# Queries' square sums as 32-column products, their roots through memory, first decay sums from a built table

## What is computed

```python
def rms_norm(x, g):
    y = xf * lax.rsqrt(jnp.mean(xf * xf, axis=-1, keepdims=True) + EPS)
    return (y * g.astype(jnp.float32)).astype(x.dtype)

# gated_deltanet
    g = -jnp.exp(a_log.astype(f32)) * jax.nn.softplus(a.astype(f32) + dt_bias.astype(f32))
    gcum = jnp.cumsum(gch, axis=-1)
    decay = jnp.exp(jnp.where(incl, gcum[..., :, None] - gcum[..., None, :], -jnp.inf))
...
# dsa_attention
    q = apply_rope(rms_norm(q.reshape(Bsz, T, B_HEADS, B_DH), q_norm), cos_a, sin_a)
    k = apply_rope(rms_norm(k.reshape(Bsz, T, 1, B_DH), k_norm), cos_a, sin_a)[:, :, 0]
```

## Time and profile before

| | us |
|---|---|
| median of 3 runs | 1572.85 |
| the three runs | 1573.34, 1567.5, 1572.85 |
| the profiled execution | 1569.99 |
| its span, first to last instruction | 1568.0 |
| TensorE busy in it | 1555.1 (99%) |
| VectorE busy | 1146.8 (73%) |
| ScalarE busy | 882.9 (56%) |
| mean granted TensorE clock | 0.997 |

### The profile page before, as it was taken

The page is one execution under the profiler, slowest core; times in us unless marked ns, Lnnn a source line. Parts: engine busy times, 40 slices in busy tenths (PEclk is TensorE's granted clock), DMA queues, the critical chain, the costliest instruction groups (busy, mean ns, idle before and its releaser), DMA issues.

```text
span 1568.0 us, 34689 instructions
## 1 busy us (share of the span) xinstructions
PE 1555.1 (99%) x12704; PEld 1522.7 (97%) x12704; DVE 1146.8 (73%) x1901; ACT 882.9 (56%) x1380; POOL 50.4 (3%) x44
## 2 busy tenths in 40 slices
PE   9999999999999999999999999999999999999999
PEld 8999899999999998999999999999999999999999
DVE  7779787766568697786765678888666757678864
ACT  6665656555455756565554565666544456466552
POOL 0100001000000000010000000000010000100000
PEclk9999999999999999999999999999999999999999
DMA  6754154655546541547655545565555545656664
GB/s 217 221 154 122 55 188 150 194 173 173 175 148 181 156 148 63 162 156 223 197 182 191 180 122 186 158 191 187 190 185 184 165 135 162 188 161 189 186 192 131
DMA packets 272878, 263.54 MB, mean 168 GB/s; under 512 B 19440, under 2 KB 271120, under 8 KB 272784
## 3 DMA queue, kind: packets, MB, share of 16 engines
q1 hardware_dynamic: 271552, 258.47, 53.0%
q0 software_dynamic: 944, 3.70, 0.8%
q10 hardware_dynamic: 288, 0.07, 0.0%
HBM read 256.38 MB, written 3.11 MB: 165 GB/s over the span
## 4 chain that ended last, share of the span: by engine, by line
PE 86%; DVE 8%; ACT 3%; issue 1%; DMA 1%; SPq 0%; DVEq 0%; ACTq 0%
PE lin L573 23%; PE lin L576 23%; PE lin L581 23%; PE aux L925 6%; PE lin L925 3%; PE lin L627 3%; DVE wL L560 2%; PE lin L598 1%; PE lin L662 1%; DMA stage<-in_w_in 1%; DVE cT L2100 1%; DVE nT L2545 1%; DVE nL L2550 1%; ACT wH L551 1%; PE aux L576 1%
## 5 line engine op out<-in xcount | busy, mean ns | idle before, releaser
L551 ACT ACTIVATE wH<-stage 128x1024 fp32r<-128x1024 f32 x488 | 493.4, 1049 | 465.6 <-PE lin L576 318.6
L560 DVE TENSOR_TENSOR wL<-stage,wH 128x1024 fp32r<-128x1024 f32 x488 | 575.7, 1223 | 133.5 <-PE lin L581 67.2
L573 PE MATMUL lin<-nH,wH 128*128 128x256 f32 (+2 forms) x2256 | 559.4, 286 | 1.8 <-DVE u L2491 1.5
L576 PE MATMUL lin<-nL,wH 128*128 128x256 f32 (+2 forms) x2256 | 555.1, 285 | 0.0
L573 PEld LDWEIGHTS lin<-nH,wH 128*128 128x128 f32 x2256 | 426.1, 189 | 5.3 <-issue 2.1
L576 PEld LDWEIGHTS lin<-nL,wH 128*128 128x128 f32 x2256 | 427.1, 189 | 0.4 <-issue 0.2
L581 PE MATMUL lin<-nH,wL 128*128 128x256 f32 (+2 forms) x2256 | 295.1, 283 | 0.0
L581 PEld LDWEIGHTS lin<-nH,wL 128*128 128x128 f32 x2256 | 281.4, 188 | 0.3
L573 PE MATMUL lin<-aH,wH 128*128 128x256 f32 (+1 forms) x704 | 172.3, 284 | 0.0
L576 PE MATMUL lin<-aL,wH 128*128 128x256 f32 (+1 forms) x704 | 172.2, 284 | 0.0
L573 PEld LDWEIGHTS lin<-aH,wH 128*128 128x128 f32 x704 | 132.8, 189 | 0.0
(11 more groups left out here) (394 smaller groups left out, 2055.9 us busy)
## 6 DMA issues: line engine op xcount, KB each, us to landing
stage<-in_w_up SPq DMA_DIRECT2D x88, 512.0 KB, 4.5
stage<-in_ffn_w_up SPq DMA_DIRECT2D x88, 512.0 KB, 4.2
stage<-in_w_in SPq DMA_DIRECT2D x52, 512.0 KB, 5.0
stage<-in_w_down SPq DMA_DIRECT2D x40, 512.0 KB, 3.6
stage<-in_ffn_w_down SPq DMA_DIRECT2D x40, 512.0 KB, 4.1
stage<-in_w_gate SPq DMA_DIRECT2D x32, 512.0 KB, 4.7
stage<-in_even_w_in SPq DMA_DIRECT2D x24, 512.0 KB, 4.6
stage<-in_w_out SPq DMA_DIRECT2D x16, 512.0 KB, 4.1
```

What stands on the lines that cost most here:

```text
L551: nc.scalar.activation(wH[:, s, ks, 0:n], stage[:, s, ks, 0:n], ACT.Copy).then_inc(sem["whi"], 1)
L560: nc.vector.tensor_tensor(wL[:, s, ks, 0:n], stage[:, s, ks, 0:n], wH[:, s, ks, 0:n].bitcast(F32), ALU.subtract).then_inc(sem["wlo"], 1)
L573: mm = nc.tensor.matmul(banks[b][0:rows_, 0:width], wH[:, s, k, cols], xh, start=start and n == 0, stop=False)
L576: mm = nc.tensor.matmul(banks[b][0:rows_, 0:width], wH[:, s, k, cols], xl, start=False, stop=False)
```

## The change

In `JOBS` the four names `sbq0` to `sbq3` become one, `sbq`: four products with 32 columns of ones, whose results lie in four groups of 32 partitions of one bank. ScalarE takes one logarithm and one exponential of that bank (into `root_late`), then the key's logarithm, then issues a DMA that stores one row per head into memory (`rows_b`), then the key's exponential. GpSimd waits for that store and issues a DMA that reads the four rows back into all 128 partitions of `rnb[:, 0:4]` (`spread`), ahead of its cosine product of the key. VectorE scales the queries behind `joined(4)`, the split and `masked(5)`, after a wait for that DMA (`roots_b`). For gb0, VectorE builds `gtri0`, the triangle times each head's `gg`, and TensorE runs one product with ones over its 64 columns.

```diff
-    + [f"sbq{h}" for h in range(4)] + ["sbk"] + ["Y_4"] + [x for b in range(3) for x in (f"kt{b}", f"vt{b}")]
+    + ["sbq", "sbk", "Y_4"] + [x for b in range(3) for x in (f"kt{b}", f"vt{b}")]
...
+            def spread(to, rows_, stored, landed):
+
+                pool.wait_ge(*stored)
+                pool.dma_start(to.rearrange("p h t -> p (h t)"), bass.AP(rows_, 0, [[0, P], [1, to.shape[1] * to.shape[2]]])).then_inc(sem[landed], 16)
...
                 for n, (kind, x) in enumerate((("i", rawT[:, 20:24, META:T]), ("i", ikr[:, :].unsqueeze(1)), ("a", bkr[:, :].unsqueeze(1)), ("a", rawT[:, 16:20, :]))):
+                    if n == 2:
+                        spread(rnb[:, 0:4, :], rows_b, (sem["stored_b"], at("stored_b", l, 16)), "roots_b")
...
+                def rows_of_squares(name, x):
+
+                    ps = begin(name, l)
+                    for h in range(4):
+                        t = mm(ps[32 * h:32 * h + 32, 0:T], ones[:, 0:32], x[:, h, :])
+                    t.then_inc(filled(name), 1)
...
+                    if b == 0:
+                        pe.wait_ge(sem["gt"], at("gt", l, 2))
+                        mm(ps[:, 0:4 * n], ones[0:n, :], gtri0.rearrange("p h c -> p (h c)")).then_inc(filled("gb0"), 1)
+                        return
...
-                for h, name in enumerate([f"sbq{h}" for h in range(4)] + ["sbk"]):
-                    mm(begin(name, l)[:, 0:T], ones, sq_att[:, h, :]).then_inc(filled(name), 1)
+                rows_of_squares("sbq", sq_att[:, 0:4])
+                mm(begin("sbk", l)[:, 0:T], ones, sq_att[:, 4, :]).then_inc(filled("sbk"), 1)
...
+                def rows_stored(to, x, n, counter):
+                    act.wait_ge(sem["roots"], at("roots", l, n))
+                    act.dma_start(bass.AP(to, 0, [[T, 4], [1, T]]), x[0:P:32, :]).then_inc(sem[counter], 16)
...
-                root_log([f"sbq{h}" for h in range(4)] + ["sbk"], rnb, 1.0 / P)
-                root("sbk", rnb, 0.0)
+                root_log(["sbq"], root_late[:, :].unsqueeze(1), 1.0 / P)
+                root("sbq", root_late[:, :], 0.0, "roots")
+                root_log(["sbk"], rnb, 1.0 / P, 4)
+                rows_stored(rows_b, root_late, 1, "stored_b")
+                root("sbk", rnb[:, 4, :], 0.0)
...
+                dve.wait_ge(sem["gt"], at("gt", l, 1))
+                v.tensor_tensor(gtri0[:, :, :], bf(const("upto", META, META), 1, [META, 4, META]), bf(gg[0:META, 0, :], 2, [META, 4, META]), ALU.mult).then_inc(sem["gt"], 1)
+                dve.wait_ge(sem["tables_in"], 32)
...
-                v.scalar_tensor_tensor(rawT[:, 16:20, :], rawT[:, 16:20, :], pc(K_QN), rnb[:, 0:4, :], ALU.mult, ALU.mult).then_inc(sem["att_unit"], 1)
                 joined(4)
                 split_lo(dve, m0 + M_GATE + 1, 0)
                 masked(5)
+                dve.wait_ge(sem["roots_b"], at("roots_b", l, 16))
+                v.scalar_tensor_tensor(rawT[:, 16:20, :], rawT[:, 16:20, :], pc(K_QN), rnb[:, 0:4, :], ALU.mult, ALU.mult).then_inc(sem["att_unit"], 1)
                 take_eight(1)
                 gate_lo(0, [1])
```

More of the change, by code:

```diff
@@ L213 @@
     "sq": DC, "rstd": 2, "n": 2 * DC, "nh": DC, "nl": DC,
-    "conv": 12, "silu": 3, "sq_heads": 2, "sq_att": 1, "sq_ik": 1, "rn": 4, "qk_unit": 2, "att_unit": 3,
-    "sp_in": 1, "sp_ln": 1, "gt": 1, "eg": 4, "dec": 3, "kdx": 1, "qe": 1,
+    "conv": 12, "silu": 3, "sq_heads": 2, "sq_att": 1, "sq_ik": 1, "rn": 4, "roots": 1, "stored_b": 16, "roots_b": 16, "qk_unit": 2, "att_unit": 3,
+    "sp_in": 1, "sp_ln": 1, "gt": 2, "eg": 4, "dec": 3, "kdx": 1, "qe": 1,
     "rates_out": 3 * 16, "rates_in": 3 * 16, "rates_exp": 1, "rope_cos": 4, "rope_sin": 4, "swapped": 2 * 4 * 16, "keys_crossed": 2 * 16, "queries_crossed": 2 * 16, "rope": 4, "score": 6, "ml": 2 * len(UPPER), "mt_out": 3 * 16, "mt_in": 3 * 16, "solved": 1, "bt_out": 2 * 16, "b_out": 3 * 16, "x_back": 2 * 16, "a_back": 3 * 16,
@@ L313, in build @@
         sqh, _ = tile("sqh", [P, DC, T], mixer_tail)
+        gtri0, _ = tile("gtri0", [META, 4, META], mixer_tail + 4 * DC * T)
         decay, _ = blocks("decay", ml_at)
@@ L329, in build @@
         za = [nc.dram_tensor("za0", (4, META + 1, META), F32)] + [nc.dram_tensor(f"za{b}", (4, P // 2 + 1, P), F32) for b in (1, 2)]
+        rows_b, = (nc.dram_tensor(f"rows_{x}", (4, T), F32) for x in "b")
         zx = [None] + [nc.dram_tensor(f"zx{b}", (4, P + 1, P), F32) for b in (1, 2)]
@@ L417, in build @@
         rsm, o = tile("rsm", [P, 3, 4], o)
+        root_late, o = tile("root_late", [P, T], o)
         aH, f_at = tile("aH", [P, FC, T], arena, F32R)
@@ L1574, in root_log, with root @@
                         f(to[:, h0 + h, :], bank(name)[:, 0:T], Ln, bias=eps_col, scale=scale).then_inc(emptied(name), 1)
-                def root(last, to, bias_):
+                def root(last, to, bias_, counter="rn"):
                     act.wait_ge(*read(last, l))
-                    f(to[:, :, :], to[:, :, :], Exp, scale=-0.5, bias=bias_).then_inc(sem["rn"], 1)
+                    f(to, to, Exp, scale=-0.5, bias=bias_).then_inc(sem[counter], 1)
+                def rows_stored(to, x, n, counter):
+                    act.wait_ge(sem["roots"], at("roots", l, n))
+                    act.dma_start(bass.AP(to, 0, [[T, 4], [1, T]]), x[0:P:32, :]).then_inc(sem[counter], 16)
                 act.wait_ge(sem["panel_done"], 2 * (m0 + 5) + 3)
@@ L1603, in layer @@
                 root_log(["sik"], rni, 1.0 / P)
-                root("ssq3", rnq, lnq_col)
-                root("ssk3", rnk, 0.0)
-                root("sik", rni, 0.0)
+                root("ssq3", rnq[:, :, :], lnq_col)
+                root("ssk3", rnk[:, :, :], 0.0)
+                root("sik", rni[:, :, :], 0.0)
                 split_hi(act, m0 + 6, 0)
```

## The result

| us | before | after |
|---|---|---|
| median (range) of 7 runs each | 1568.57 (1567.32 to 1573.34) | 1576.50 (1574.08 to 1577.98) |
| ratio to before, 95% interval | | 1.0049 [1.0038, 1.0061] |
| profiled execution | 1569.99 | 1577.98 |
| its span | 1568.0 | 1575.9 |
| its mean granted clock | 0.997 | 0.995 |

The changed kernel is 7.9 us slower, 0.5%. The three runs of before that stood ahead of the prediction (median 1572.85) lay 4.3 us above the median of the longer series, so two numbers have to be held apart: the forecast time, 1577.8, is 1.3 us from the measured one, but the forecast difference, +5.0, was 2.9 too small. That the time came out so near is luck: the high start and the small difference cancel.

A forecast was written before the change was run, and what follows sets the result against it. TensorE, busy nearly throughout, was taken to bound the kernel. Layers at +1.63 us each gave +3.3, and one clock fall of 1.7 made +5.0; on the median of 1572.85 that gave 1577.8 us, range 1571 to 1582.

The forecast's parts named there:

- The chain and the stand: Join of level 5: the moved scaling delays T_5's read, so TensorE stands 3.1 us in layer 0, 3.4 in layer 1.
- Square sums: TensorE's square sums of the queries: 1.16 us off the stream, of which 0.76 is left at the join of level 4.
- gb0: First decay sums on TensorE: eight 16-column records become two of 64 columns, −0.67 us per layer.
- Roots: Queries' roots through memory: there at 133 to 133.5 us, bounds 132.9 and 136.7, ahead of the moved scaling.
- the memory rule: GpSimd's DMA issue: VectorE can lock it out of its descriptors' memory; the issue might wait one split operation more, still covered.
- Clock: Thin stretches at TensorE's stands: one short fall to half speed in the two layers, adding 1.7 us.
- slower rival: Clock falls at both layers' stands and stays down 6.8 us each: +10.1 us, 1582.9; chance 0.13.
- The layers' sum at full clock: Both layers without clock falls: +1.63 us each, together +3.3.
- onto the sine product, which VectorE can spare: GpSimd's cosine product of the queries moves off a VectorE split of 4.62 us and onto the sine product, harmlessly.

The follow-up runs named there:

- e1: The changed kernel with the wait for the spread roots and the queries' scaling back at their old place behind the key's scaling; 1570.00 us, ratio 1.0014.
- e2: The changed kernel with SyncE issuing gate panel 2's first half ahead of the wait for the scaled queries and the crossing; 1573.08 us, ratio 1.0023.
- e4: The kernel before with only the scaling of the queries moved behind masked(5); 1580.27 us, ratio 1.0062.
- e11: The changed kernel with ScalarE reading Y_5 and T_5 ahead of its split of gate panel 2's first half; 1573.65 us, ratio 1.0024.
- e3: The kernel before with the gb0 part alone: the built table and one 64-column product in place of four of 16; 1566.22 us, ratio 0.9987.
- e7: e2 with VectorE's sine product of the queries moved to right before its sum; 1570.04 us, ratio 1.0006.
- e12: e7 with the copy of the first state S moved from VectorE to ScalarE; 1567.08 us, ratio 0.9979.
- e9: e7 with two of the four top-k rounds left out on VectorE in each layer, so the selection differs; 1564.56 us, ratio 0.9964.
- e10: e3 with two of the four top-k rounds left out on VectorE in each layer, so the selection differs; 1566.93 us, ratio 0.9984.
- e5: The kernel before with gate panel 2's first half issued ahead of the wait for the scaled queries and the crossing; 1576.53 us, ratio 1.0048.

## Where the prediction was right and where it was wrong

- **The chain and the stand: right.** The join waited 2.8 and 3.2 us for ScalarE's read (forecast 3.1 and 3.4), behind crossing, panel and split. From the sums to the join TensorE lost 2.1 us in layer 0 and 2.9 in layer 1 (join +8.69 less sums +5.76), forecast 2.3 and 2.6. e1, e2, e4 and e11 each confirm a link.
- **Where it was wrong within the chain.** The scaling ended at 134.8, not 137.3. Two terms: I reckoned from start times of before, and let VectorE come 0.3 us sooner to the last read of the `kt` banks, but it came 2.6 sooner with TensorE (128.41 against 130.98); and masked(5) took 0.75 us in place of 1.33, with no product of GpSimd beside it. A new wait at joined(4) gives 0.4 back. In the sum these mostly cancel: T_5 was read by 146.64, not 148.7, and TensorE would have been there at 143.91, not 145.64.
- **Square sums: right in layer 0, not in layer 1.** 1.14 us off the stream (forecast 1.16); the eight records of the queries start in two rounds of four, 0.23 us apart, at 123.40 and 123.65, as forecast. In layer 0, 0.34 of it is given back by the join of level 4 (forecast 0.40). In layer 1 all but 0.07 is given back: sums 560.96 before and 566.72 after, +5.76, join of level 4 567.09 and 572.79, +5.70. Two new waits take it (timeline of TensorE, after, layer 1), the longer one for VectorE's read of the bank, the place that I had named and priced by layer 0 alone:

```profile
568.33 0.69 PE L935 MATMUL aux<-X,ML 128*64 128x64 f32 x16 [0.29 <-DMA X<-zx]
...
571.76 1.09 PE L1142 MATMUL aux<-c,cT 128*128 128x128 f32 x8 [0.90 <-DVE kd L2300]
```

  The Trainium skill ("TensorE: Matmul & The Clock Gate", Measured speedup vs the span model) would have made the gain 0.1 smaller; the trace does not show that.
- **gb0: right.** −0.80 in layer 0's trace, of which 0.14 was there at 80.7 us already, ahead of gb0, so −0.66; −0.55 a layer at full clock in e3; forecast −0.67. The fall of the clock behind it did go, which I had priced at 0.
- **Roots: right in what hangs on them, 2 us late in time.** VectorE waits for no DMA ahead of the scaling; e1, which wanted them 2 us sooner, waited. The spread was issued at 127.07 and took 3.9 us in the median, so the roots were there near 131, not at 133 to 133.5. ScalarE's issue took 1.06 us in place of the 0.6 that I took from SyncE's, and it was hidden. No issue held by VectorE showed up, so the memory rule of the Trainium skill ("DMA: Bandwidth & Descriptors", SWDGE vs HWDGE vs iDMA) changed nothing. That section ties the rule to one mode of VectorE, the 2-port one, which the prediction left out; no run here shows in which mode the split works.
- **Clock: the step that failed, by its account.** I took one short fall, 1.7 us, and no more. The profiled execution has three (3.4, 6.8 and 6.8 us), and loses two of before. Over all runs the net is 1.9 to 3.3 us; that the 1.7 comes near its lower end is luck. I had counted only falls added by the two stands: the two that vanish (one behind gb0, one at 602.2) and the one that arises at 167.7, 20 us behind the first, were not in the sum. In the slower rival I had set both falls at 6.8 and none of before gone; the net lies between it and the forecast.
- **The layers' sum at full clock: 4.4 measured, 3.3 forecast.** With what the trace and e3 show for its terms, 2.1 + 2.9 − 2 × 0.55 − 0.3, it would be 3.6. The remaining 0.8 is about the standard error of the difference (0.7); it stays open. Of the 2.9 us that the forecast difference lacked, 1.1 are at full clock, 0.2 to 1.6 are clock, and the rest comes of comparing medians of 7 runs with means of longer series.
- **A claim that failed without moving this time: that GpSimd's cosine product goes "onto the sine product, which VectorE can spare".** Rows of VectorE before, layer 0, then of VectorE and GpSimd after:

```profile
145.54 0.43 DVE L2115 TENSOR_TENSOR bkr<-bkr,bk_s 128x272 f32<-128x272 f32 x1
```

```profile
140.75 1.29 DVE L2150 TENSOR_TENSOR tmp<-tmp,c 128x1088 f32<-128x1088 f32 x1 [1.31 <-DMA tmp<-rawT]
141.96 2.76 DVE L2143 TENSOR_TENSOR bkr<-bkr,bk_s 128x272 f32<-128x272 f32 x1
```

```profile
137.57 2.50 POOL L911 TENSOR_TENSOR bkr<-bkr,c 128x272 f32<-128x272 f32 x1 [9.89 <-DMA bk_s<-bkr]
140.79 3.62 POOL L911 TENSOR_TENSOR rawT<-rawT,c 128x1088 f32<-128x1088 f32 x1 [0.72 <-DMA tmp<-rawT]
```

After, VectorE waits 1.3 us for the crossed queries, and its sum of the keys takes 2.76 us beside GpSimd's product of the queries, ending 0.3 us behind it (144.72 and 144.41); before, the same sum took 0.43 with GpSimd idle. TensorE's stand at the join hides this in after. With the chain mended it is part of what TensorE waited for in e2: e7 took the wait away and won 1.5 us at full clock. e12, with the copy of S gone from VectorE too, is another 0.6 lower, with an error of 0.4.

## What to carry to other kernels

When an operation moves back on one engine, follow every in-order queue that waits for it: here 1.5 us on VectorE moved a crossing, by the crossing a weight panel, by the panel a split, and by the split a small read that could have been made nearly 8 us sooner, and only that read was on the path. A gain on the busy engine counts only as far as the next fullest engine has room; try the relief of that engine together with the gain (e9) and without it (e10), since either alone may show nothing. The cost of an edit depends on what else is changed (the move cost 5.2 us alone and 2.3 on top of the rest, at full clock), so build a change up in more than one order. And price a stand of some 3 us with the half-speed stretch that may follow, but also look which falls of the clock the edit removes.

## What was unexpected of the hardware

- Four fp32 products of 32 columns side by side take the time of one: their records start within 0.02 us, and the next round 0.23 us later, as one 128-column record takes. Each change of form costs 0.1 more (0.32 in place of 0.23), so the sums' ten records went from 2.39 us to 1.25 and not to 0.92.
- Small transfers issued right behind a panel's loads on the same queue could be used after 7.5 and 6.8 us, with a median of 2.0 where no panel goes ahead (e5, before); that the queue is the cause is not shown.
- VectorE and GpSimd beside each other: after, GpSimd's product of 128x272 took 2.50 us beside VectorE's split, in place of 0.86, while the split kept its 2.35; and VectorE's sum of 128x272 took 2.76 beside GpSimd's product of 128x1088, in place of 0.43. The same neighbourhood had shown in the earlier trace rows as a split of 4.62 in place of 2.36.
- Falls of the clock wander with the stands: after had them at 147, 167 and 591 us, and e4, which shares only the moved scaling with it, at 147, 171, 591 and 615; e11, with waits of 1.5 and 1.6 us, had none in its profiled execution, though over all its runs it lost 5.3 us to the clock.
